# Two transformer blocks on one core: post-norms and the gated mixture turned token tile by token tile, the last quarter inside the next product

## What is computed

```
m = sigmoid(g_pool) * y_pool + sigmoid(g_attn) * y_attn     # gated mixture
h = h + rmsnorm(m @ w_out, norm_mix_post)                   # post-norm 0
u2 = rmsnorm(h, norm_mlp_pre)
a = square(relu(u2 @ w_up))
h = h + rmsnorm(a @ w_down, norm_mlp_post)                  # post-norm 1
x = h; x = x + 0.5 * swiglu(rmsnorm_2(x, g_ffn1), ...)      # first product of the second block
...
y = concat(rmsnorm_2(y_conv), rmsnorm_2(y_att))             # two sums of squares, ysum and osum
```

## Time and profile before

| | us |
|---|---|
| median of three runs | 1507.57 |
| the profiled execution | 1507.48 |
| its span (first to last record) | 1505.7 |
| TensorE busy with matmuls | 1495.8 (99%) |
| TensorE busy with weight loads | 1288.3 (86%) |
| VectorE busy | 1020.7 (68%) |
| ScalarE busy | 785.1 (52%) |
| mean granted TensorE clock | 0.999 |

### The profile page before, as it was taken

The page is one execution under the profiler, slowest core; times in us unless marked ns, Lnnn a source line. Parts: engine busy times, 40 slices in busy tenths (PEclk is TensorE's granted clock), DMA queues, the critical chain, the costliest instruction groups (busy, mean ns, idle before and its releaser), DMA issues.

```text
span 1505.7 us, 20960 instructions
## 1 busy us (share of the span) xinstructions
PE 1495.8 (99%) x8178; PEld 1288.3 (86%) x8178; DVE 1020.7 (68%) x1101; ACT 785.1 (52%) x899; POOL 54.7 (4%) x81
## 2 busy tenths in 40 slices
PE   9999999999999999999999999999999999999998
PEld 8878888888888888889888888888888888888886
DVE  5666766657566677987666667666567896676656
ACT  4554644446444465646544446444446655554444
POOL 0200100001000000010100001000000010000000
PEclk9999999999999999999999999999999999999999
DMA  9546455554555555353555455555545354355553
GB/s 375 201 146 246 168 190 184 184 195 168 195 191 175 213 197 175 141 195 112 196 190 189 179 195 196 199 191 195 191 172 200 137 195 168 112 196 195 188 191 124
DMA packets 40507, 280.44 MB, mean 186 GB/s; under 512 B 4608, under 2 KB 4864, under 8 KB 7040
## 3 DMA queue, kind: packets, MB, share of 16 engines
q1 hardware_dynamic: 39440, 275.08, 50.9%
q10 hardware_dynamic: 1008, 4.53, 0.8%
HBM read 277.49 MB, written 2.10 MB: 186 GB/s over the span
## 4 chain that ended last, share of the span: by engine, by line
PE 93%; DVE 5%; ACT 1%; issue 0%; DMA 0%; POOL 0%; SPq 0%; POOLq 0%; DVEq 0%; ACTq 0%
PE ps L399 90%; DVE w_lo L1514 2%; PE ps L624 1%; PE ps L616 1%; DVE accT L2014 0%; PE ps L666 0%; ACT Pb L1074 0%; DVE sT_lo L1521 0%; DMA raw<-stream_in 0%; DVE cu L2060 0%; DVE cu L2062 0%; ACT w_hi L1021 0%; DVE Pb L1547 0%; PE ps L970 0%; DVE Pb L1566 0%
## 5 line engine op out<-in xcount | busy, mean ns | idle before, releaser
L1514 DVE TENSOR_TENSOR w_lo<-raw,w_hi 128x2048 fp32r<-128x2048 f32 x250 | 571.5, 2290 | 256.0 <-ACT w_hi L1021 255.6
L1021 ACT ACTIVATE w_hi<-raw 128x2048 fp32r<-128x2048 f32 x251 | 479.8, 1914 | 291.2 <-PE ps L399 280.1
L399 PE MATMUL ps<-xT,w_hi 128*128 128x512 f32 (+1 forms) x2488 | 588.7, 378 | 0.0
L399 PEld LDWEIGHTS ps<-xT,w_hi 128*128 128x128 f32 x2488 | 444.5, 189 | 76.7 <-issue 0.2
L399 PE MATMUL ps<-xT,w_lo 128*128 128x256 f32 x2304 | 330.4, 282 | 0.0
L399 PEld LDWEIGHTS ps<-xT,w_lo 128*128 128x128 f32 x2304 | 314.9, 191 | 16.5
L399 PE MATMUL ps<-w_hi,sT_hi 128*128 128x512 f32 x576 | 186.2, 391 | 0.0
L399 PE MATMUL ps<-w_lo,sT_hi 128*128 128x512 f32 x576 | 185.5, 390 | 0.0
L399 PE MATMUL ps<-w_hi,sT_lo 128*128 128x512 f32 x576 | 185.3, 389 | 0.0
L399 PE MATMUL ps<-w_hi,xT 128*128 128x512 f32 x576 | 173.7, 392 | 1.3 <-ACT w_hi L1115 1.0
L399 PEld LDWEIGHTS ps<-w_hi,xT 128*128 128x128 f32 x576 | 107.7, 188 | 26.7 <-issue 3.2
(11 more groups left out here) (201 smaller groups left out, 932.0 us busy)
## 6 DMA issues: line engine op xcount, KB each, us to landing
raw<-stream_in SPq DMA_DIRECT2D x255, 1024.0 KB, 4.8
raw<-stream_in SPq DMA_DIRECT2D x4, 256.0 KB, 5.4
kTx<-mem_in SPq DMA_DIRECT2D x1, 1024.0 KB, 12.2
cu<-gate_bias_in SPq DMA_DIRECT2D x1, 1024.0 KB, 14.1
qk_tok<-post_gain_in ACTq DMA_DIRECT2D x1, 1024.0 KB, 5.2
kTx<-mem_in ACTq DMA_DIRECT2D x1, 1024.0 KB, 6.8
mem_kept<-kTx ACTq DMA_DIRECT2D x1, 1024.0 KB, 4.3
kTx<-mem_kept ACTq DMA_DIRECT2D x1, 1024.0 KB, 4.7
```

What stands on the lines that cost most here:

```text
L399: return nc.tensor.matmul(bank_ap, lh, rh, start=start, stop=stop)
L1021: nc.scalar.activation(w_hi[:, slot(c), 0:width], raw[:, slot(c), 0:width], copy).then_inc(unit_hi, 1)
L1514: nc.vector.tensor_tensor(w_lo[:, slot(c), :], raw[:, slot(c), :], w_hi[:, slot(c), :].bitcast(F32), sub).then_inc(unit_lo, 1)
```

## The change

It has three parts.

1. *Post-norms 0 and 1.* The last unit of the product, the sums, GpSimd's statistic, the gain and the addition go in the order BY_TOKEN. The addition of quarter (0,1) is split in two instructions of 256 columns, the first counted on a new semaphore post_piece. TensorE's `turn_post` runs two small products instead of three and turns (0,0), (1,0), and (0,1) in two pieces; the quarter (1,1) is turned by `turn_post_last` between part 0 and part 1 of the next `merged`. The waits and the order of `turn_round` and `turn_rest` and of what stands behind them are not edited.
2. *The gated mixture.* TensorE turns three quarters, waits for m2q3 (which frees bank 7), multiplies unit 20, turns the fourth quarter, and goes on with unit 21. ScalarE's and VectorE's programs are not edited here.
3. *A rest between two sums.* In both layers VectorE's rest of unit 20 goes ahead of osum.

GpSimd's statistic at the very end becomes a call of the common function, with the same instructions.

```diff
-WARM_X, WARM_FIRST, WARM_NORM = 4, 2, 3
+WARM_X, WARM_FIRST, WARM_NORM = 4, 2, 2
...
+            def turn_post(n):
+
+                warm(WARM_NORM)
+                pe.wait_ge(res_ready, 4 * n + 1)
+                turn_part(res, U, 0, 0, (0, 4))
+                pe.wait_ge(mem_ready, n + 1)
+                pe.wait_ge(res_ready, 4 * n + 2)
+                turn_part(res, U, 1, 0, (0, 4))
+                pe.wait_ge(post_piece, n + 1)
+                turn_part(res, U, 0, 1, (0, 2))
+                pe.wait_ge(res_ready, 4 * n + 3)
+                turn_part(res, U, 0, 1, (2, 4))
+
+            def turn_post_last(n):
+
+                pe.wait_ge(res_ready, 4 * n + 4)
+                turn_part(res, U, 1, 1, (0, 4))
...
-            for q in range(4):
+            def mixed_turned(q):
                 pe.wait_ge(b_dve.sem, BB(f"mh{q}"))
                 turn_part(m_tok, (0, 1, 2, 3), q // TOK, q % TOK, (0, 4))
+
+            for q in range(3):
+                mixed_turned(q)
+            pe.wait_ge(b_dve.sem, BB("m2q3"))
             for i in range(4):
-                tall(0, 20 + i, 2 * i, 4, i == 0, i == 3, xT_hi, xT_lo, tiles=BT)
+                tall(0, 20 + i, 2 * i, 4, i == 0, i == 3, xT_hi, xT_lo, tiles=BT, order=BY_TOKEN)
+                if i == 0:
+                    mixed_turned(3)
...
             turn_mem(0)
-            warm(WARM_NORM)
-            turn_res(U, 0, 1)
+            turn_post(0)
...
                     merged(r3, c, 0, 4, tiles)
+                    turn_post_last(0)
                     merged(r3, c + 1, 1, 4, tiles, half_done)
...
             turn_mem(1)
-            warm(WARM_NORM)
+            turn_post(1)
...
                             merged(r3, c, 0, 4, tiles)
+                            if by_post:
+                                turn_post_last(1)
                             merged(r3, c + 1, 1, 4, tiles, gate_done)
...
                 scaled(0)
-                scaled(1)
-                did1(scaled(2), f"{name}a")
+                did1(scaled(1), f"{name}a")
                 dve.wait_ge(post_rstd, post_done(n, 0))
                 wait_own1(f"{name}a")
-                onto(0)
+                onto(0).then_inc(res_ready, 1)
+                onto(1).then_inc(res_ready, 1)
+                scaled(2)
                 did1(scaled(3), f"{name}b")
                 dve.wait_ge(post_rstd, post_done(n, 1))
-                onto(1)
-                onto(2)
                 wait_own1(f"{name}b")
-                onto(3)
+                onto(2, 0, 256).then_inc(post_piece, 1)
+                onto(2, 256, 512).then_inc(res_ready, 1)
+                onto(3).then_inc(res_ready, 1)
...
                 did(nc.vector.tensor_reduce(ysum, ysq.rearrange("p c n -> p n c"), AX.X, add), "ysum")
+                unit(20)
                 wait_act("osq3")
                 did(nc.vector.tensor_reduce(osum, osq.rearrange("p c n -> p n c"), AX.X, add), "osum")
-                unit(20)
...
-                both, done = stat[:, T_MIX, 0:2], 5 * n
-                pool.wait_ge(sums, before + 2)
-                nc.gpsimd.tensor_tensor(both, part[:, 0:2], consts2[:, 2, :], ALU.add).then_inc(post_rstd, 1)
-                pool.wait_ge(post_rstd, done + 1)
                 for t in range(TOK):
-                    mean, inv = stat[:, T_MIX, 2 + t:3 + t], rs(T_MIX, t)
-                    pool.wait_ge(sums, before + 3 + t)
-                    nc.gpsimd.tensor_tensor(mean, stat[:, T_MIX, t:t + 1], part[:, 2 + t:3 + t], ALU.add).then_inc(post_rstd, 1)
-                    pool.wait_ge(post_rstd, done + 2 * t + 2)
+                    inv = rs(T_MIX, t)
+                    both, mean = stat[:, T_MIX, t:t + 1], stat[:, T_MIX, 2 + t:3 + t]
+                    pool.wait_ge(sums, before + 2 * t + 1)
+                    nc.gpsimd.tensor_tensor(both, part[:, 2 * t:2 * t + 1], consts2[:, 2, 0:1], ALU.add).then_inc(post_rstd, 1)
+                    pool.wait_ge(post_rstd, post_done(n, t) - 2)
+                    pool.wait_ge(sums, before + 2 * t + 2)
+                    nc.gpsimd.tensor_tensor(mean, both, part[:, 2 * t + 1:2 * t + 2], ALU.add).then_inc(post_rstd, 1)
+                    pool.wait_ge(post_rstd, post_done(n, t) - 1)
                     nc.gpsimd.tensor_tensor(inv, mean, consts2[:, 3, 0:1], ALU.pow).then_inc(post_rstd, 1)
```

More of the change, by code:

```diff
@@ L244, in program @@
         post_rstd = sem("post_rstd")
+        post_piece = sem("post_piece")
         mem_T, mem_ready, mem_saved = sem("mem_T"), sem("mem_ready"), sem("mem_saved")
@@ L269, in post_done @@
         def post_done(n, t):
[L271 to L275 removed]
+            return 6 * n + 3 * (t + 1)
         def rstd_done(i):
@@ L627, in turn_part, with turn_res @@
                         last.then_inc(turn_T, 1)
-            def turn_res(banks, before, post=None):
+            def turn_post(n):
[12 more added lines that the diff above has]
+                turn_part(res, U, 1, 1, (0, 4))
+            def turn_res(banks, before):
                 for half in range(2):
                     for t in range(TOK):
-                        if post is not None and (half, t) == (1, 0):
-                            pe.wait_ge(mem_ready, post)
                         pe.wait_ge(res_ready, before + 2 * half + t + 1)
@@ L784, in down1 @@
                 tall(r3, c, tile, 4, start, False, sT_hi, sT_lo)
-                tall(r3, c + 1, tile + 2, 4, False, stop, sT_hi, sT_lo)
+                tall(r3, c + 1, tile + 2, 4, False, stop, sT_hi, sT_lo, order=BY_TOKEN)
             c0 = B1_UNITS - B1_MLP
@@ L811, in ffn @@
                     before = res_of(l, -1 if which == 0 else 2)
-                    turn_res(U, before - 4, 2 if l == 0 and which == 0 else None)
+                    by_post = l == 0 and which == 0
+                    if not by_post:
+                        turn_res(U, before - 4)
                     tl = turns_before(l, 0 if which == 0 else 5)
@@ L1050, in product_squares @@
             def product_squares(i, last_unit, before):
-                for q in range(4):
+                for q, (half, t) in enumerate(BY_TOKEN):
                     if q < 3:
@@ L1057, in product_squares @@
                     act.wait_ge(sums, before + q)
-                    nc.scalar.activation(scratch[:, 0:512], ps[:, 4 + q, :], square, scale=D ** -0.5,
+                    nc.scalar.activation(scratch[:, 0:512], ps[:, 4 + 2 * half + t, :], square, scale=D ** -0.5,
                                          accum_out=part[:, q:q + 1]).then_inc(sums, 1)
@@ L1498, in _ @@
                 act.wait_ge(fin_gain, 2 * t + 1)
-                act.wait_ge(post_rstd, last_done(t))
+                act.wait_ge(post_rstd, post_done(2, t))
                 o = out_tok[:, t, 0:512]
@@ L1711, in scaled, with onto @@
                 def scaled(q):
-                    half = q // TOK
+                    half, t = BY_TOKEN[q]
                     dve.wait_ge(sums, before + q + 1)
[L1714 to L1719, removed]
+                    return nc.vector.tensor_tensor(Pb[:, q, :], ps[:, 4 + 2 * half + t, :],
+                                                   gain[:, half * 512:half * 512 + 512], mul)
+                def onto(q, c0=0, c1=512):
+                    half, t = BY_TOKEN[q]
+                    r = res[:, t, half * 512 + c0:half * 512 + c1]
+                    return stt(out=r, in0=Pb[:, q, c0:c1], scalar=rs(T_MIX, t), in1=r, op0=mul, op1=add)
                 dve.wait_ge(gpost_in, 16)
                 scaled(0)
-                scaled(1)
-                did1(scaled(2), f"{name}a")
+                did1(scaled(1), f"{name}a")
                 dve.wait_ge(post_rstd, post_done(n, 0))
                 wait_own1(f"{name}a")
-                onto(0)
+                onto(0).then_inc(res_ready, 1)
+                onto(1).then_inc(res_ready, 1)
+                scaled(2)
                 did1(scaled(3), f"{name}b")
                 dve.wait_ge(post_rstd, post_done(n, 1))
-                onto(1)
-                onto(2)
                 wait_own1(f"{name}b")
-                onto(3)
+                onto(2, 0, 256).then_inc(post_piece, 1)
+                onto(2, 256, 512).then_inc(res_ready, 1)
+                onto(3).then_inc(res_ready, 1)
             post_norm(0, gpost[:, 0:D], "postmix", 4)
@@ L2228, in _ @@
                     statistic(in_layer(l, i), tile, width)
[L2229 to L2239, removed]
+            post_statistic(2, sums_of(LAYERS, 0) - 2)
 def _wide(w):
```

4 lines of the change are left out of this document (2 added, 2 removed).

## The result

The changed kernel takes 1526.34 us (1526.26 to 1527.26), the kernel before 1507.68 (1507.49 to 1507.79): a ratio of 1.0126, 95% interval 1.0114 to 1.0138, or 18.7 us more. The profiled execution took 1526.26, with a span of 1524.5 and a mean granted clock of 0.994. The forecast was 1522.2, its range ended at 1526.

A forecast was written before the change was run, and what follows sets the result against it. TensorE's instructions and the holes between them were taken to bound the kernel. 1507.48 + 4.8 + 4.7 + 4.7 - 1.1 = 1520.6, plus 1.6 for one clock fall, gave 1522.2 us, range 1519 to 1526.

The forecast's parts named there:

- What bounds the kernel, and which way it goes: Whole kernel: TensorE's instructions and the holes between them set the end, so each standstill is paid in full; slower.
- The mixture's stall: Gated mixture: unit 21 waits for its rest behind VectorE's turn_rest, starting at 145.6 instead of 140.8, +4.8 us.
- The post-norms' stalls: Post-norms 0 and 1: part 1 waits for a rest queued behind the fourth quarter's remainders, +4.7 us each.
- The sums: Two layers: unit 20's rest ahead of osum removes TensorE's 0.57 us wait in each, -1.1 us.
- The clock: Three idle stretches of 4.4 and 4.7 us: one fall to half speed taken, 1.6 us, bounds 0 and 4.8.
- The sum: Whole kernel: 1507.48 + 4.8 + 4.7 + 4.7 - 1.1 = 1520.6, with one clock fall 1522.2 us.
- turn only: All three places: the rest is covered, TensorE waits for remainders alone; 0.5 us and 2.5 twice, 1511.9 us; chance 0.05.
- Not slower: All three places: split turns work as meant; +0.5 in the mixture, -0.06 twice, -1.1, 1506.8 us; chance 0.04.
- Clock stays down: All three stretches: the clock falls, each slow spell twice the start's, 3 x 3.3 = 9.9 us, 1530.5; chance 0.08.

The follow-up runs named there:

- the last two kernels: Changed kernel, post-norms' fourth turn mid part 0, rest before third pair, mixture as before: 1507.08 us; post-norm turns before product, mixture's fourth behind unit 20, rest moved: 1506.36 us.

## Why the prediction was wrong, point by point

- **What bounds the kernel, and which way it goes:** right. TensorE is the bound, and each stall is paid in full.
- **The mixture's stall:** right. Forecast 4.8, measured 4.80; the turn at 140.72 (140.8), ScalarE at 141.37 (141.45), VectorE at 142.00 and 143.20 (142.1, 143.4), unit 21 at 145.54 (145.6).
- **The post-norms' stalls:** right, a little low. Forecast 4.7 each, net of the earlier start; measured 5.31 - 0.45 = 4.86 and 5.31 - 0.36 = 4.95. The part that was short is the earlier start (0.55 forecast) and the gap from turn to part 1 (5.31 us from 173.32, 5.2 forecast).
- **The sums:** right, -1.1 forecast, -0.9 in the trace and -1.0 by itself.
- **The clock:** this term was mis-sized, and it is what put the time outside the range. The failed step is "I take one fall", 1.6 us, with 4.8 as the bound for three. All three came, in the profiled execution and by the mean clock of 0.993 or 0.994 in the others too, and cost 1.49, 2.03 and 1.54 us, 5.1 together: 3.5 more than was taken. The reason given, that 4.4 to 4.7 us is only just over the 3.6 at the program's end, read one fall as if it were the least idleness that brings it. The traces show no such number. At the second hole the clock fell 2.2 us after the last matmul, and the same fall at the program's end came 2.4 us after it in one trace (eight products filled in, 1512.8 to 1515.2) and 4.7 us in another (the turn early, 1498.5 to 1503.2). The bound was too low as well, by a little: the slow stretch of post-norm 0 lasted 4.5 us of work, not the 3.3 seen at the start. That the point of a fall differs from one to the next, as the sentence beside the sum has it, is so; that some of the three would not come is not, in these four runs.
- **The sum:** 14.2 - 1.1 + 1.6 forecast, 14.7 - 0.9 + 5.1 measured. Had all three falls been in it at 1.6, it would have read 1525.4; the 0.9 left are small misses of the same sign in every term.
- **The rivals:** "turn only" is what the kernel with the rests moved shows, 1511.9 forecast for it and 1512.6 to 1515.8 measured; its condition was not given in the changed kernel. "Not slower" put its price of the idea with free queues at +0.5 and -0.06 twice; the last two kernels show +0.4 in the mixture and some +0.6 a post-norm over turning all four first, since there the turn fits in a wait. "Clock stays down" was right in that all three falls came, and wrong in its price, 3.3 us each against 1.5 to 2.0. In one execution of the kernel with the mixture undone a fall cost 2.8, which is near that price.

## What to carry to other kernels

Before moving a step of one engine later, list what is queued behind its consumers on every other engine: the loops that wait for it hold up whatever stands behind them, here a weight rest that had nothing to do with the turn and made 8.5 of the 13.9 us of holes. Ask too whether the step lies in a wait: a turn that fills a hole costs nothing, and costs its full length wherever else it is put. And where a change opens holes in TensorE's stream, count one fall of the clock for every hole like the 4.2 and 4.8 us ones here, and for holes near 3 us give a range that has none of the falls at one end and all at the other.

## What the runs showed of the hardware

- Holes of 4.2 and 4.8 us brought a fall of the granted clock to 1.2 GHz each time, by the traces of two kernels (five falls at five holes) and the times of their other runs. Holes of 3.1, 3.7 and 3.7 us brought three in one execution and at most one in each of two others. With holes of up to 2.0 us there was none.
- The fall came 2.2 us after TensorE's last matmul in one hole and up to 1.3 us after TensorE had gone on behind others. At the program's end it came 2.4 to 4.7 us after the last matmul in the twelve traces.
- A fall cost 1.5 to 2.8 us here: 3.4 to 6.0 us of work at half speed.
- In kernels with holes near 3 us, runs of the same kernel differ by up to 3.8 us; in those with none over 2 us, by 0.3 to 0.8.
- float32 transposes kept the clock at full as well as matmuls: 26 in each hole gave 1521.24 us, 16 small matmuls 1521.46, neither 1526.34.
